# Paired 1024-row modulation units, the pair in each stage end, and VectorE's order there

## What is computed

```python
def adaln(cond, w, b):
    m = jax.nn.silu(cond) @ w + b            # w: 2048 x 12288 per layer
    return [m.reshape(cond.shape[0], 6, 1, D_MODEL)[:, j] for j in range(6)]

# in each layer, for context and for latents
h = rmsnorm(x, g0) * (1 + sc1) + sh1
x = x + g1 * rmsnorm(mixer(h) @ w_o, g1n)
h = rmsnorm(x, g2) * (1 + sc2) + sh2
x = x + g2 * rmsnorm(square(relu(h @ w1)) @ w2, g3n)
```

## Time and profile before

| | us |
|---|---|
| median of 3 runs | 2574.95 |
| lowest, highest | 2572.07, 2575.25 |
| the profiled execution | 2574.7 |
| its span | 2572.9 |

### The profile page before, as it was taken

One profiled execution on the slowest core, in us unless ns is written; L12 is line 12 of the kernel. 1 busy time (PEld: TensorE's weight loads), 2 busy tenths in 40 slices (PEclk: granted clock), 3 DMA queues, 4 the chain that ended last, 5 costly groups with the idle time before them and its releaser, 6 DMA issues.

```text
span 2572.9 us, 37557 instructions
## 1 busy us (share of the span) xinstructions
PE 2508.4 (97%) x14850; PEld 2027.9 (79%) x14850; DVE 1366.2 (53%) x1496; ACT 1052.7 (41%) x1148; POOL 114.6 (4%) x164
## 2 busy tenths in 40 slices
PE   6899999989999999999999999999899999999998
PEld 3578888778878878878777877897787888888887
DVE  2244445475545536536555454564765464564665
ACT  3223344363334333423353365583533333343342
POOL 0020000000000000000000032200000000000000
PEclk8999999999999999999999999999999999999999
DMA  9988988958878878878787754559588555555554
GB/s 361 360 271 287 291 287 285 348 174 277 294 252 272 281 243 279 278 259 264 265 300 266 251 179 159 166 169 334 179 260 288 183 187 205 166 193 197 184 196 175
DMA packets 497463, 634.54 MB, mean 247 GB/s; under 512 B 12128, under 2 KB 378512, under 8 KB 496080
## 3 DMA queue, kind: packets, MB, share of 16 engines
q1 hardware_dynamic: 488672, 608.46, 70.9%
q0 software_dynamic: 6352, 23.31, 2.6%
q10 hardware_dynamic: 2336, 1.31, 0.2%
HBM read 623.90 MB, written 9.13 MB: 246 GB/s over the span
## 4 chain that ended last, share of the span: by engine, by line
PE 80%; DMA 10%; DVE 5%; ACT 3%; issue 1%; SPq 0%; POOL 0%; ACTq 0%; DVEq 0%
PE PS L1256 23%; PE PS L1257 12%; PE PS L1324 10%; PE PS L1326 10%; PE PS L1325 10%; PE PS L1283 4%; DVE WLO L1816 3%; ACT WHI L1560 2%; DMA RAW<-in_w_qkvg_gla 2%; DMA RAW<-in_w_o_na 2%; DMA RAW<-in_w_mlp 2%; DMA RAW<-in_w_o_gla 2%; PE PS L1265 2%; PE PS L1267 1%; PE PS L1266 1%; DMA SCR<-in_w_ada 1%
## 5 line engine op out<-in xcount | busy, mean ns | idle before, releaser
L1816 DVE TENSOR_TENSOR WLO<-RAW,WHI 128x2048 fp32r<-128x2048 f32 x384 | 878.8, 2300 | 767.0 <-ACT WHI L1560 762.2
L1560 ACT ACTIVATE WHI<-RAW 128x2048 fp32r<-128x2048 f32 x384 | 731.7, 1915 | 729.7 <-DMA RAW<-in_w_mlp 484.8
L1256 PE MATMUL PS<-HM,WHI 128*128 128x512 f32 x2560 | 913.8, 401 | 7.3 <-DVE SCR L2053 3.5
L1257 PE MATMUL PS<-HM,WLO 128*128 128x256 f32 x2560 | 718.5, 281 | 0.0
L1256 PEld LDWEIGHTS PS<-HM,WHI 128*128 128x128 f32 x2560 | 482.2, 188 | 139.3 <-issue 18.4
L1257 PEld LDWEIGHTS PS<-HM,WLO 128*128 128x128 f32 x2560 | 484.6, 189 | 0.2
L1324 PE MATMUL PS<-WHI,HID 128*128 128x512 f32 x1152 | 453.9, 394 | 6.0 <-DVE WLO L1816 6.0
L1325 PE MATMUL PS<-WLO,HID 128*128 128x512 f32 x1152 | 449.6, 390 | 0.0
L1326 PE MATMUL PS<-WHI,HID 128*128 128x512 f32 x1152 | 449.2, 390 | 0.0
L1324 PEld LDWEIGHTS PS<-WHI,HID 128*128 128x128 f32 x1152 | 216.8, 188 | 63.6 <-issue 19.3
L1326 PEld LDWEIGHTS PS<-WHI,HID 128*128 128x128 f32 x1152 | 216.8, 188 | 45.9
(11 more groups left out here) (238 smaller groups left out, 1882.4 us busy)
## 6 DMA issues: line engine op xcount, KB each, us to landing
RAW<-in_w_mlp SPq DMA_DIRECT2D x256, 1024.0 KB, 5.8
ADW<-in_w_ada SPq DMA_DIRECT2D x176, 1024.0 KB, 8.5
RAW<-in_w_qkv_na SPq DMA_DIRECT2D x48, 1024.0 KB, 6.8
RAW<-in_w_qkvg_gla SPq DMA_DIRECT2D x32, 1024.0 KB, 6.4
SCR<-in_w_ada SPq DMA_DIRECT2D x16, 1024.0 KB, 11.3
RAW<-in_w_o_na SPq DMA_DIRECT2D x16, 1024.0 KB, 7.1
RAW<-in_w_qkvg_gla SPq DMA_DIRECT2D x32, 512.0 KB, 4.8
RAW<-in_w_o_gla SPq DMA_DIRECT2D x16, 1024.0 KB, 7.0
```

Of the source, the lines that this page charges most:

```text
L1256: mm(bank[:, 0:2 * T2], hi[:, k, cols], act[:, kc, 0:2 * T2], start=first, stop=False)
L1257: return mm(bank[:, 0:T2], lo[:, k, cols], act[:, kc, 0:T2], start=False, stop=last)
L1560: actv(WHI[:, 2 * s + u, 0:n], RAW[:, u, 0:n], ACT.Copy).then_inc(hi_done, 1)
L1816: tt(WLO[:, 2 * s + u, 0:n], RAW[:, u, 0:n], WHI[:, 2 * s + u, 0:n].bitcast(f32), ALU.subtract).then_inc(lo_done, 1)
```

## The change

Five things are altered.

1. A unit has 1024 rows and 512 columns. Two consecutive ones (even and odd) make a pair that adds up in one PSUM bank. A unit takes 8 matmuls of 512 columns, its DMAs have rows of 2 KB.
2. ScalarE copies and stores a pair in two halves of 256 columns (`row_half`, `copy_half`, `store_half`), once it is complete, with two buffers and two semaphores `row_out`.
3. The units are laid out anew. Before: 18, 6 + 1 in the stage end, 4 x 9, 1, 6, 4, 1, 7. After: 18, 6 + 2, 4 x 10, 2, 4, 2, 2, 4. `with_between` places both loads of a stage end's pair in the last output slab's plan, and `turn_rest` runs the first ahead of the transposes and the second after those of the context.
4. In hidden slabs of the MLPs each quarter of 512 rows is multiplied for bank 0 and then for bank 1.
5. VectorE splits half 1 of the next slab ahead of the latent half's `stream_norm`, and orders modulations and low parts as 0, 1, low 0, low 1, 2, 3, low 2, low 3. ScalarE does modulation 2 and 3, both copies, the high parts 0 to 3, and then the stores.

```diff
-        PLAN_WO0, PLAN_WO, PLAN_V = ((0, 1), (2, 3), (4, 5), ()), ((0,), (1,), (2, 3), ()), ((0, 1), (2, 3), (4,), (5,))
-        PLAN_MLP = {GU: ((0,), (1,), (2, 3), (4,)), LU: ((0,), (1,), (2,), ())}
+        PLAN_WO0, PLAN_WO, PLAN_V = ((0, 1), (2, 3), (4, 5), ()), ((0,), (1,), (), ()), ((0,), (1,), (2,), (3,))
+        PLAN_MLP = {GU: ((0, 1), (2, 3), (4, 5), ()), NB: ((), (), (), ())}
...
                 for u in range(2):
                     sp.wait_ge(ada0_used if u == 0 else ada_done, a + 1)
-                    src = w_ada[layer, u * UNIT_ROWS:(u + 1) * UNIT_ROWS, ds(col, UC)] \
-                        .rearrange("(c p) n -> p c n", p=P)
-                    sp.dma_start(ADW[:, u, :].rearrange("p (c n) -> p c n", c=UKC), src).then_inc(ada_in[u], 16)
+                    row = UNIT_ROWS * odd + YC * u
+                    src = w_ada[layer, row:row + YC, ds(col, AC)].rearrange("(c p) n -> p c n", p=P)
+                    sp.dma_start(ADW[:, u, :].rearrange("p (c n) -> p c n", c=4), src).then_inc(ada_in[u], 16)
...
             def with_between(plan, n):
-                return plan[n] + ((max(map(max, filter(None, plan))) + 1,) if n == YN - 1 else ())
+                last = max(map(max, filter(None, plan)))
+                return plan[n] + ((last + 1, last + 2) if n == YN - 1 else ())
...
+                if quarter:
+                    for part in range(2):
+                        quarter(2 * u + part)
+                        for b in range(2):
+                            if u == 0 and part == 0:
+                                pe.wait_ge(bank_free, m * 2 + b + 1)
+                            for k in range(4 * part, 4 * part + 4):
+                                end = body(MAIN[2 * s + b], hi, lo, b, UKC * u + k, k, u == 0 and k == 0,
+                                           u == 1 and k == UKC - 1)
...
             def turn_rest(f, m0):
+                first = BETWEEN[f - 1]
+                pe.wait_ge(bank_free, evacuated(m0, YN - 2, 1))
+                ada_rows(first, 0, BETWEEN_ROWB)
                 turn_stream(f, 0, range(2, 4))
-                pe.wait_ge(bank_free, evacuated(m0, YN - 2, 1))
-                ada_rows(BETWEEN[f - 1], BETWEEN_ROWB)
+                ada_rows(first + 1, 1, BETWEEN_ROWB)
                 turn_stream(f, 1, range(4))
-                pe.wait_ge(row_ready, BETWEEN[f - 1] + 1)
+                pe.wait_ge(row_ready, first + 2)
...
                 if f < 3:
-                    ada_row(BETWEEN[f], False, BETWEEN_ROWB)
                     modulate(f + 1, shift, 2)
-                    store_row(BETWEEN[f])
-                    modulated_hi(f + 1, 0)
                     modulate(f + 1, shift, 3)
-                    for g in range(1, 4):
+                    copy_half(BETWEEN[f], 0, MROW[:, :], BETWEEN_ROWB)
+                    copy_half(BETWEEN[f], 1, MROW_LATER, BETWEEN_ROWB)
+                    for g in range(4):
                         modulated_hi(f + 1, g)
+                    store_half(BETWEEN[f], 0, MROW[:, :])
+                    store_half(BETWEEN[f], 1, MROW_LATER)
...
                 split_lo(m0 + 2 * YN, 0, UNIT, (0,))
                 residual(f, 2, 0)
                 residual(f, 3, 0)
+                split_lo(m0 + 2 * YN, 0, UNIT, (1,))
                 stream_norm(m0, f, 1, add)
...
-                    if g:
-                        modulated_lo(f + 1, g - 1)
-                    if g == 2:
-                        split_lo(m0 + 2 * YN, 0, UNIT, (1,))
+                    if g == 1:
+                        modulated_lo(f + 1, 0)
+                        modulated_lo(f + 1, 1)
+                modulated_lo(f + 1, 2)
                 modulated_lo(f + 1, 3)
```

More of the change, by code:

```diff
@@ L877, in gla_vector @@
             link(nc.vector.memset(DEC2, 1.0))
-            dve.wait_ge(row_out, rows_stored(A_WO1))
+            for half in range(2):
+                dve.wait_ge(row_out[half], rows_stored(A_WO1))
             def log_gates(n):
@@ L1503, in mlp_group @@
             def mlp_group(g, layer, m, a, f, per, norm=None):
-                with pe.Fori(0, NB) as i:
-                    for s in range(2):
-                        slab = g * (4 * NB) + i * 2 + (m + s)
-                        ada = g * per + i + a if s == 0 and a is not None else None
-                        step(slab, s, features_out(HM), ada, filled(f), modulated(2 * layer + 1))
+                with pe.Fori(0, NB // 2) as pair:
+                    for x in range(2):
+                        for s in range(2):
+                            slab = g * (4 * NB) + pair * 4 + (m + 2 * x + s)
+                            ada = g * per + pair * 2 + (a + x) if s == 0 and a is not None else None
+                            step(slab, s, features_out(HM), ada, x, filled(f), modulated(2 * layer + 1))
                 for n in range(YN):
@@ L1644, in out_slab @@
                     out_squares(m0, f, n - 1)
-                for a in ada[:1]:
-                    ada_row(a)
-                    store_row(a)
+                if pair is not None and not pair[1]:
+                    row_half(pair[0], 0)
                 if f is not None and n == YN - 1:
@@ L1652, in out_slab @@
                     split_hi(m + 2, 0, UNIT, range(2), keys)
-                for a in ada[1:]:
-                    ada_row(a)
-                    store_row(a)
+                if pair is not None and pair[1]:
+                    row_half(pair[0], 0)
                 if 0 < n < YN - 1:
                     more_squares(f, (("x0",), ("x1",))[n - 1])
+                if pair is not None:
+                    row_half(pair[0], 1)
             def start_squares():
@@ L1764, in mlp @@
                 first = 1 if last else 0
-                per = LU if last else GU
+                per = NB if last else GU
                 if last:
@@ L1773, in mlp_group @@
             def mlp_group(g, layer, m, a, per, complete=False, last=False):
-                with act.Fori(0, NB) as i:
-                    for s in range(2):
-                        slab = g * (4 * NB) + i * 2 + (m + s)
-                        ada = g * per + i + a if s == 0 and a is not None else None
-                        step(slab, s, ada, (g * KC + i * 4 + (layer * HID_GROUPS * KC + 2 * s), i, s))
+                with act.Fori(0, NB // 2) as two:
+                    for x in range(2):
+                        for s in range(2):
+                            slab = g * (4 * NB) + two * 4 + (m + 2 * x + s)
+                            pair = g * per + two * 2 + a if x and a is not None else None
+                            step(slab, s, pair, (g * KC + two * 8 + (layer * HID_GROUPS * KC + 4 * x + 2 * s),
+                                                 two * 2 + x, s))
                 m0 = g * (4 * NB) + (m + 2 * NB)
```

175 lines of the change are left out of this document (87 added, 88 removed).

## The result

The changed kernel takes 2660.8 us (median; 2657.1 to 2663.8), the kernel before 2575.1 us (2572.1 to 2575.4) beside it: a ratio of 1.0335, with a 95% interval of 1.0317 to 1.0353. The forecast was 2624.4 us with a range of 2603 to 2642. The sign was right, the size was not: the kernel is 36 us slower than forecast and lies outside the range.

What follows compares the result with a forecast made beforehand. TensorE, busy 97% of the span, was taken to bound the kernel, leaving its 64.5 us of idle and half-clock stretches to win or lose. 2574.7 + 58.5 + 3 - 6.2 - 4.6 - 1 = 2624.4 us, range 2603 to 2642.

Steps and rivals of the forecast that it cites:

- step 5: Quarter order and VectorE's order: -1 us, from TensorE's waits for second quarters; attention's copies and stores: 0.
- step 4: Fewer loads under output slabs: -4.6 us in all; GLA output -5.1, first MLP's last slab +1.5, attention output -1.
- Step 1: Stage ends: the pair's second load holds the next slab on SyncE's queue, 19.5 us an end, +58.5 us.
- Step 2: Stage ends: TensorE at half clock after idling, 1 us an end, +3 us.
- Rival A: SyncE's order is harmless and the slab is not held up: 2565.2 us, faster; chance 5%.
- B: Slab held at stage ends, but its load lands as on idle queues, 15.4 us an end: 2609 us; chance 15%.
- C: Slab held at stage ends and the following slabs of the next stage starve too: 2645 us; chance 7%.
- Step 3: Three units moved from TensorE-bound stages into idle time at stage ends, 2.06 us each: -6.2 us.

Runs made afterwards that it cites:

- the two queue experiments: Changed kernel, each with one move: the pair's first unit consumed inside the last output slab, 2604.2 us; the second unit's load requested behind the next stage's first slab, 2620.0 us.
- the last experiment: Changed kernel with first unit inside the last output slab, attention's stores behind the split and MLP 0's groups written out on TensorE: 2570.0 us, ratio 0.9977.
- the third experiment: Changed kernel with attention's four stores of a pair issued behind the high split of the next slab's first half: 2642.1 us, ratio 1.026.

## Why the prediction was right in its sign and wrong in its size

Three terms make the miss of 36.4 us: step 5's 0 for attention's copies and stores (18.7 us measured), no term at all for the longer loop body on TensorE (12.1 us), and step 4's +1.5 for the first MLP's last slab (some 5 us).

**Step 1 (+58.5): right. Step 2 (+3): too large.** The chain came out in its order and nearly to the microsecond: RAW requested at T+2.8 (forecast T+2.8), first copy T+13.0 (T+12.4), second T+15.8 (T+15.4), evacuation T+20.7 (T+20.2 by the list, T+19.7 with its 0.5 us for the wider rows), first matmul T+31.8 (T+31.3 by steps 1 and 2 together). Three ends cost 60.6 us by the two traces against 61.5. They can be split at the evacuation. It is 20.5, 19.2 and 20.3 us later than before, 60.0 in all, which is step 1. From there to the first matmul it takes 11.15, 10.72 and 10.70 us where it took 10.62, 10.73 and 10.63: 0.6 us in all, which is what the half clock cost in the ends, and step 2 had 3. The half clock fell on the transposes at each end and on the second unit at the first only. So the sum of the two steps is closer than its terms, which is in part luck. Rival A (the queue is harmless) is void: the two queue experiments show that the slab behind the load makes the price. B (15.4 us an end) and C (the following slabs starve) are out too: 20 us an end, and in the first 40 us of the new stages no matmul but the very first waits.

**Step 3 (-6.2): not contradicted.** The second MLP has three units fewer and is 6.6 us shorter. It also has the other form of the units, the pairs in its loop body and the quarter order, so this is no measurement of the units alone.

**Step 4 (-4.6): right for GLA, wrong for the first MLP.** The GLA stretch is 13.4 us shorter where four units and step 4's -5.1 make 13.3. The attention output's gain of 1 us can't be told: its wait is 3.82 to 3.88 us in four kernels with the old units, and 2.90, 3.21, 3.94 and 4.06 in four with the new ones and this plan; T varies by more.

The wide rows do carry more: in attention (170 to 410 us) the DMA engines move 293 GB/s at a share of 0.91 in the kernel before and 292 at 0.87 in the changed one with its stores moved, so 322 and 336 at full share (half of what is loaded there has the wide rows), where the forecast's working has 324 and 353 for narrow and wide. In the whole program, 608.46 MB took 70.9% of 2572.9 us before, which is 1824 us of the DMA engines' time, and 69.5% of 2565.0 us, 1783 us, in the last experiment. The Trainium skill's page "DMA: Bandwidth & Descriptors", section Specifications, has line rate from 512 B on, by which this would be no difference; the measured one is 2%, small, but not none, and in the direction that the term took.

The term that fell is the first MLP's last slab: 3.96 us of idle against 1.79, 1.7 us for the 12 matmuls at half clock behind it, and 1.33 us of waiting for an ADW load 30 us ahead of it. That is 5.2 us, and not the +1.5 that was taken; even the upper bound was 4.6. The variants with the same plan wait 3.11, 3.78 and 4.28 us there. The text said that the shorter ADW loads bring it down; in that stage they didn't, and the slab that already had this plan was the nearer row.

**Step 5 (-1): here the forecast failed most.** It said "In attention the copies and stores come every second slab: 0". The stores cost 18.7 us by experiment. The step weighed how many copies and stores there are and not where they stand on their queue. Its general sentence, that the copies "sit behind splits but ahead of what TensorE needs them for", holds for the long stages and not for attention, where the change puts row_half, with its stores, ahead of split_hi (the removed lines of the third experiment's edit). With 0.57 us an issue, four issues a pair and 8 pairs (some 16 units, 15.3 us apart), the working would have given 8 x 4 x 0.57 = 18 us. The quarter order is worth nothing that can be measured, and VectorE's order, alone in the kernel before, neither.

**What no step had.** The change doubles a loop body on TensorE, and the forecast counted only its columns. A jump back over a whole group cost some 3 us of idle for a load of instructions, at one of the two jumps a second gap, and some time at half clock: 12.1 us in the changed kernel and 15.8 in the kernel before with only this done to it. No row of the trace of before shows such a gap, so the edit had no nearest row; it should have been named as an unknown with a bound, and was taken at nothing.

The sum, again by the traces: forecast 2624.4; attention +24.8, the first MLP +14.5, the rest -0.4; this gives the 2663.2 us of the profiled execution to 0.1. Of the 24.8 the stores' edit explains 18.7. The trace of that edit has T at 547.2, 25 us earlier and within the 545.6 to 549.7 of the old units, and the three traces that differ only behind that point span 5 us, so the remainder is of the size by which executions differ. Of the first MLP's 14.5 the written-out loop explains 10 and the last slab 3.7. Open is from which length of body on TensorE pays for the jump: the second MLP's groups have the same pairs without units, and show no gap, nor a packet of the instruction queue from 2269 to 2475 us, around the jump back there.

## What to carry to other kernels

Before a load is moved or added on an in-order queue, write down what is queued behind it and when the buffer it needs is freed: a load that waits for a consumer behind a stage boundary takes the next stage's first data with it, here at 20 us a boundary. Read each DMA issue of a compute engine as an instruction of 0.57 us in that engine's order; it was free beside a running split, and ahead of one on a chain four of them and a copy delayed it by 3 us, of which 2.3 came through. When a loop body is made longer, look in the new trace for idle time at the jump back (put down to "issue", or to a releaser that is no wait in the old trace), and for packets of the instruction queue beside it. Before a unit of filling is moved, look for a wait that it can fill: right ahead of a wait it cost next to nothing here.

## What the hardware showed that was not expected

TensorE idled 3.20 and 3.29 us at the jump back over a long group, and a shorter gap (0.78 us here, 0.89 to 2.22 us in other kernels with the long body) often followed some 4 to 5 us later. A packet of the instruction queue starts beside each of these gaps, and TensorE goes on 3.1 to 3.3 us after it at the jump and 2.3 to 2.5 us after it at the second gap. With the loop written out the gaps were gone at the same number of matmuls, and the instruction queue moved 86 packets instead of 92. In the kernel before, whose body is half as long, the queue moved none for 413 us of repeated groups.

The clock behind such a gap is not always the same. In the changed kernel the granted clock stayed at 1.00 for the 3 us after the first gap, and was 0.53, which is the 1.2 GHz level for nearly all of it, in the 3 us after the second.
